# Reordering the mixers' element-wise work, the sample columns' convolution and the first attention loads in a hybrid decoder step

## What is computed

```python
h = rmsnorm(x); z = h @ w_in            # columns shared out among the mixers
# A forgetting attention, 4 heads x 64: causal for the prompt, and over 8192 paged keys for the samples
s = q @ k.T * scale + c_q - c_k         # c = cumsum(log forget gate)
# B RWKV-7: xm = sh + rw_mu * (prev - sh), r, k, v, w, a from xm, kk = k*rw_kk
kk = kk * rsqrt(max(sum(kk*kk), 1e-12)) # per head, then a scan with a matrix state
# C causal pooling with windows 2/4/8/16
# D glu = u1 * sigmoid(u2); y = depthwise conv (31 taps) + conv_b
yn = (y - mean) * rsqrt(var + 1e-5) * ln_g + ln_b
out = silu(yn) @ pw_out
x = x + concat(each mixer * silu(its gate)) @ w_out; y = rmsnorm(x)
```

## Time and profile before

| | |
|---|---|
| median of 3 runs | 1674.64 us (1670.19 to 1675.73) |
| the profiled execution: its time | 1666.86 us |
| its span from the first instruction to the last | 1665.1 us |
| mean granted clock of PE | 0.976 |
| PE busy | 1553.4 us, 93% |
| DVE busy | 987.7 us, 59% |
| ACT busy | 602.8 us, 36% |

### The profile page before, as it was taken

How to read it: one execution, slowest core, us unless ns; L and a number is a source line. 1 busy time by engine, 2 the same in 40 slices (tenths; PEclk the granted TensorE clock), 3 DMA queues, 4 the chain that set the end, 5 groups by cost and what they waited for, 6 DMA issues and landing times.

```text
span 1665.1 us, 35933 instructions
## 1 busy us (share of the span) xinstructions
PE 1553.4 (93%) x14428; PEld 1152.3 (69%) x14428; DVE 987.7 (59%) x2382; ACT 602.8 (36%) x1235; POOL 82.1 (5%) x97
## 2 busy tenths in 40 slices
PE   7979999999999999997777999998999999999998
PEld 5867778888887888886644666667887865444443
DVE  5689764767457666678375666634554549333333
ACT  3234342443434441334444565543333353010001
POOL 1010000000000000000000000000000003222220
PEclk9999999999999999999879999999999999999999
DMA  6354473446544374344758746668575559999983
GB/s 225 116 189 160 163 280 129 154 142 235 198 134 158 111 262 143 112 159 157 237 197 241 198 142 187 176 202 245 170 220 177 185 197 357 358 337 353 354 314 132
DMA packets 184495, 341.71 MB, mean 205 GB/s; under 512 B 22213, under 2 KB 124101, under 8 KB 173638
## 3 DMA queue, kind: packets, MB, share of 16 engines
q1 hardware_dynamic: 167338, 256.88, 47.3%
q0 software_dynamic: 10496, 72.98, 11.7%
q10 hardware_dynamic: 6496, 9.56, 1.5%
HBM read 286.13 MB, written 55.35 MB: 205 GB/s over the span
## 4 chain that ended last, share of the span: by engine, by line
PE 45%; ACT 3%; DMA 2%; issue 1%; DVE 1%; SPq 1%; ACTq 0%; DVEq 0%
PE psum L1323 24%; PE psum L1017 5%; PE psum L1269 4%; PE psum L1197 4%; PE psum L1283 4%; PE psum L1628 2%; PE psum L1044 1%; PE psum L1531 1%; DMA big<-lfD 1%; DMA big<-zT 1%; ACT big L1712 1%; PE psum L1031 1%; SPq L817 0%; DMA big<-rkv 0%; ACT big L1964 0%
## 5 line engine op out<-in xcount | busy, mean ns | idle before, releaser
L1044 PE MATMUL psum<-big 128*128 128x256 f32 (+1 forms) x1920 | 438.7, 386 | 11.2 <-DVE big L2085 9.3
L1044 PEld LDWEIGHTS psum<-big 128*128 128x128 f32 x1920 | 367.3, 192 | 70.4 <-DVE big L2085 10.1
L1725 ACT ACTIVATE zst<-psum 128x256 f32<-128x256 f32 (+1 forms) x336 | 126.7, 384 | 442.5 <-PE psum L1044 440.5
L1323 PE MATMUL psum<-big 64*64 64x64 f32 (+4 forms) x5440 | 256.1, 270 | 16.0 <-issue 9.3
L1323 PEld LDWEIGHTS psum<-big 64*64 64x64 f32 (+2 forms) x5440 | 176.8, 131 | 100.8 <-issue 74.7
L1044 PE MATMUL psum<-big,wbuf 128*128 128x256 f32 (+1 forms) x768 | 181.3, 384 | 0.0
L1044 PEld LDWEIGHTS psum<-big,wbuf 128*128 128x128 f32 x768 | 146.2, 191 | 23.0 <-issue 0.4
L2269 DVE SCALAR_TENSOR_TENSOR big<-big,pars 128x512 f32<-128x512 f32 x240 | 161.0, 744 | 0.4
L979 POOL DMA_INDIRECT big<-in_cache_v,pidx x64 | 68.2, 1065 | 687.3 <-PE psum L1283 474.1
L1197 PE MATMUL psum<-big 64*128 64x512 f32 (+3 forms) x320 | 74.9, 578 | 18.4 <-DMA big<-zT 12.3
L1712 ACT ACTIVATE big<-big 128x512 f32<-128x512 f32 (+11 forms) x108 | 83.9, 803 | 11.2 <-DVE big L2345 7.5
(11 more groups left out here) (322 smaller groups left out, 2028.7 us busy)
## 6 DMA issues: line engine op xcount, KB each, us to landing
big<-in_k_pages SPq DMA_DIRECT2D x432, 128.0 KB, 2.3
big<-wS SPq DMA_DIRECT2D x36, 768.0 KB, 5.8
zst<-in_k_pages SPq DMA_DIRECT2D x80, 128.0 KB, 2.7
wS<-big SPq DMA_DIRECT2D x12, 768.0 KB, 5.7
wbuf<-in_w_pairs SPq DMA_DIRECT2D x18, 512.0 KB, 3.9
big<-in_w_pairs SPq DMA_DIRECT2D x18, 512.0 KB, 4.4
...
```

Source lines behind the costliest of these rows:

```text
L1044: last = nc.tensor.matmul(psum[:, bank, 0:wide(p) // 2], left(k), right(k), start=first and k == 0, stop=k == 3, skip_group_check=True)
L1323: return nc.tensor.matmul(out, l, r, start=start, stop=stop, skip_group_check=True)
L1725: nc.scalar.activation(parts_[:, U % 2, COPIED_TO[j], 0:n], psum[:, (0, 1, 2, 0, 1, 2, 3)[j], 0:n], ACT.Copy, scale=0.125 if i == U_QA els ...
```

## The change

It does five things. (1) Token shift: the term mu*prev is made by ACT (`shifted`, two Copy with a scale per row tensor, in the unit after), DVE keeps one multiply-add per row (`mix_pair` with `one_m_mu`) and does it after the unit's taps. (2) ACT also takes the gain of the next pass's inputs (a Copy with a scale of 512 columns in units 2 to 9; `normed` becomes two wide multiplications), the key norms' floor (`key_sums`, a Relu) and small copies for the samples; the Sigmoid of U_U2 comes after the first copy of unit 3, `lora_inputs` moves from unit 3 to unit 5. (3) The samples' convolution moves from pass 0, unit 3 to pass 1, unit 1 and is normalised with pass 1. (4) Pass 3 has its mean after unit 8 and its variance after unit 10 as the other passes, its state steps one unit earlier, `conv_root(3)` and `conv_silu(3)` inside unit 11, ahead of its last copies; `TAPS` is shared out anew. (5) The first attention loads are issued by SP in unit 10 of pass 3; `conv_gated(3)` comes after the first item's row maxima; `KEYS_AT` begins 10, 12, 14 in place of 8, 11, 13, `forget_sums` 0 and 1 come in items 7 and 10 in place of 5 and 7, and POOL's stores wait for later items. Rows of `ek` are ordered anew (`EK_ROWS`) so that the first loads find free rows.

```diff
-        MEAN_AT, VAR_AT = (8, 8, 8, 9), (10, 10, 10, 11)
+        MEAN_AT, VAR_AT = 8, 10
-        KEYS_AT = (8, 11, 13, 15, 17, 19, 21, 22, 23, 24, 25, 26, 27, 28, 29, 30)
+        KEYS_AT = (10, 12, 14, 16, 18, 20, 21, 22, 23, 24, 25, 26, 27, 28, 29, 30)
-        TAPS = ((0, 0, 5, 4, 4, 4, 6, 8, 0), (0, 0, 5, 4, 4, 4, 6, 8, 0), (0, 0, 5, 4, 4, 4, 6, 8, 0), (0, 0, 1, 1, 5, 5, 6, 7, 6))
+        TAPS = ((0, 0, 4, 4, 4, 4, 7, 8), (0, 0, 4, 5, 5, 5, 6, 6), (0, 0, 4, 5, 5, 5, 6, 6), (0, 0, 1, 5, 6, 7, 6, 6))
...
+            def first_columns():
+                sp.wait_ge(z_stored[0], z_stores(0, U_KA))
+                sp.wait_ge(z_stored[1], z_stores(0, U_QA))
+                sp.wait_ge(pool_stored, stores(3))
+                sp.wait_ge(v_stored, stores(3))
+                sp.wait_ge(nc_kept, 16)
+                sp.wait_ge(rw_stored, 128 * PASSES - 64)
+                kq_load(0, kq_in)
+                sp.dma_start(ck_first, ncD[:, 0:512].unsqueeze(0).to_broadcast([P, 4, 512])).then_inc(ck_in[0], 16)
...
                     if i == 10:
-                        store_scan_rows(p, 1)
                         if p + 1 < PASSES:
                             sp.wait_ge(pool_stored, stores(p))
                             wvf_load(p + 1, 1)
+                        if p == PASSES - 1:
+                            first_columns()
+                        store_scan_rows(p, 1)
...
+            pool.wait_ge(o_read, 9)
+            pool.dma_start(O['vE'], vtok[:, :, 0:256]).then_inc(st_stored, 16)
...
             for x in range(2):
+                pool.wait_ge(o_read, 12 + 2 * x)
                 pool.dma_start(O['kT'][x], zT[KA + x]).then_inc(st_stored, 16)
...
+            def key_sums(p):
+                for t in TILES:
+                    for h in HALVES:
+                        a_(kinv[:, t, half(p, h)], of_small(('key', p, t, h))[:, 0:wide(p) // 2], ACT.Relu, sr_act, bias=under)
+
+            def shifted(p, i):
+                act.wait_ge(z_add, adds_through(p, i))
+                act.wait_ge(halo_in, 3 * p + i - U_R + 1)
+                for r in range(2):
+                    a_(sig_w[:, r, 0:PT_W], ek[:, EK_ROWS[i - U_R] + r, 0:PT_W], ACT.Copy, mu_ready, scale=par7[:, 8 + 2 * (i - U_R) + r:9 + 2 * (i - U_R) + r])
...
             def lora_gates(p):
+                act.wait_ge(sh_done, mixed_through(p, MIX_V))
...
             def unit(p, i):
-                copies(p, i, 0, 2)
+                if i == 6:
+                    key_sums(p)
+                copies(p, i, 0, 1)
+                if i == 3:
+                    gate(p, U_U2, ACT.Sigmoid, u2d)
+                copies(p, i, 1, 2)
...
-                if i == 3:
-                    lora_inputs(p)
+                if i in (4, 5, 6):
+                    shifted(p, i - 1)
                 copies(p, i, 2, 3)
...
-                if i == 3:
-                    gate(p, U_U2, ACT.Sigmoid, u2d)
+                if i == 5:
+                    lora_inputs(p)
...
-                if i == 11 and p < 3:
+                if i == 11:
                     conv_root(p)
                 copies(p, i, 5, 6)
+                if 2 <= i < 2 + KT and p + 1 < PASSES:
+                    row = hb[(p + 1) % 2][:, i - 2, 0:PT_W]
+                    a_(row, row, ACT.Copy, gained, scale=par7[:, i - 2:i - 1])
...
+                if i == 11 and p == 3:
+                    conv_silu(p)
                 copies(p, i, 6, 7)
...
             def normed(p):
                 dve.wait_ge(rs_ready, 2 * p + 2)
+                dve.wait_ge(gained, KT * p)
                 for h in HALVES:
-                    for k in range(KT):
-                        row = hb[p % 2][:, k, half(p, h)]
-                        ins = v.scalar_tensor_tensor(row, row, par7[:, k:k + 1], rs[h], ALU.mult, ALU.mult)
-                        ch.mark(ins)
+                    row = hb[p % 2][:, :, half(p, h)]
+                    ch.mark(v.tensor_tensor(row, row, rs[h].unsqueeze(1).to_broadcast([P, KT, PT_W // 2]), ALU.mult))
...
             def mix_pair(p, i):
-                mix(p, 2 * (i - U_R), 2, sig_w[:, :, 0:PT_W])
+                at, n = EK_ROWS[i - U_R], 2 * (i - U_R)
+                dve.wait_ge(mu_ready, 2 * (3 * p + i - U_R + 1))
+                for r in range(2):
+                    row = ek[:, at + r, 1:1 + PT_W]
+                    v.scalar_tensor_tensor(row, row, one_m_mu[:, n + r:n + r + 1], sig_w[:, r, 0:PT_W], ALU.mult, ALU.add).then_inc(sh_done, 1)
...
                     if i in (3, 4, 5):
-                        mix_pair(p, i)
-                    if i == 3 and p == 0:
-                        sample_taps(0)
-                        sample_taps(1)
+                        mix_kept(p, i)
...
-                    if 2 <= i <= 8:
+                    if 2 <= i <= 7:
                         taps_at(p, i)
-                    if i == 8 and MEAN_AT[p] == 8:
+                    if i in (3, 4, 5):
+                        mix_pair(p, i)
+                    if i == 8:
                         centered(p)
...
-                    if j in (5, 7):
-                        forget_sums((j - 5) // 2)
+                    if j in (7, 10):
+                        forget_sums((j - 7) // 3)
```

264 lines of the change are left out of this document (144 added, 120 removed).

## The result

| | before | after |
|---|---|---|
| median | 1672.41 us (4 runs, 1664.34 to 1675.73) | 1627.35 us (4 runs, 1624.30 to 1629.30) |
| ratio to before | | 0.9736, 95% interval 0.9705 to 0.9766 |
| profiled execution | 1666.86 us | 1629.3 us |
| its span, PE's mean granted clock | 1665.1 us, 0.976 | 1627.4 us, 0.987 |

A forecast was written before the change was run, and what follows sets the result against it. PE, busy 93% of the span, was taken as the bound, so only its idle stretches and low clocks could be won: 9.6 + 4.0 - 0.9 + 1.2 + 9.0 + 7.6 + 11.1 = 41.6 us, forecasting 1633 us from the median, range 1614 to 1652.

The forecast's parts named there:

- Pass 0: Units 4 and 5: earlier Sigmoid and less DVE work remove holes of 2.59 and 6.67 us and low clock; net 9.6 us.
- Mean of pass 0: Pass 0's mean: unit 7 keeps 8 taps, its sums come later, hole 3.0 in place of 2.1: -0.9 us.
- Value weights: Their load, issued before the scan-row stores, removes the 2.88 us hole and 1.5 of low clock, less 0.4: 4.0 us.
- Passes 1 and 2: Means gain 2.0 us per pass, key norms wait about 1.4 per pass: +4.0 - 2.8 = 1.2 us.
- Pass 3: Earlier mean removes its 9.29 us hole and low clock, together 11.15, less 1.1 and a key wait of 1.0: 9.0 us.
- Start: Start of attention: early loads hidden, ACT's tail awaited instead; first transposes 12.8 us after PE's last product, not 20.4: 7.6 us.
- Items 5 to 12: Attention: waits of 5.64 us (forget rows) and 7.01 (key pages) go, 1.5 given back: 11.1 us, bounds 5 to 15.
- Rival (b): Attention: pages' wait moves to items 12 and 14, 1.5 us in each of six early steps: 1645; chance 0.10.
- (a): Projection: ACT-DVE handoffs cost 4 us more in each of four passes: 1649; chance 0.13.
- (c): Start of attention: `first_columns` held by a wait until unit 11 ends, 7.6 us less gain: 1641; chance 0.04.
- (d): Projection: ACT becomes the bound, PE pays its 35 us of added work; slower, 1687; chance 0.05.
- The list of holes: PE's idle stretches over 0.7 us in projection and attention, those that matter listed with releasers and summed to 52 us.

The follow-up runs named there:

- Experiment 1: Kernel before with unit 3's Sigmoid behind its first copy and one tap of pass 0 moved from unit 2 to unit 6: 1667.78 us, ratio 0.9965.
- Experiment 9: Changed kernel with the second part of the value weights' load put back behind the second tile's scan-row stores: 1634.43 us, ratio to before 0.9781.
- experiment 7: Changed kernel with taps 4, 4, 4, 6, 7, 6 in pass 0 and 5, 5, 4, 5, 6, 6 in passes 1 and 2: 1625.56 us.
- experiment 5: Changed kernel with ACT's list of pass 3's last unit reordered, and first scores waiting only for the first five copies: 1622.01 us, ratio to before 0.9706.
- experiment 4: Changed kernel with the loads of attention's first columns put back behind the projection: 1633.84 us, ratio to before 0.9778.
- experiment 6: Changed kernel with one unused 128 x 1 Sigmoid in ACT's unit 6 of every pass, loading the table early: 1621.54 us, ratio to before 0.9686.
- experiment 2: Kernel before with attention's items alone moved (key steps from item 10, first forget sums in items 7 and 10): 1660.37 us, ratio 0.9922.
- experiment 3: Changed kernel with attention's items put back (key steps from item 8, first forget sums in items 5 and 7): 1634.45 us, ratio to before 0.9777.
- experiment 10: Changed kernel with each of ACT's added shifts done twice, DVE's multiply-adds waiting for the second: 1627.80 us, ratio to before 0.9741.

## Why the prediction was right

**Pass 0 (9.6 predicted, 11.0 measured).** Experiment 1 shows the mechanism, one queue on DVE. The deductions came as summed: of 1.2 us for what ACT would be late with, 0.56 appeared in unit 4 and 0.68 at the low-rank products (1.45 for 0.77). Of the 1.4 us too many, 0.9 were there already when unit 4 began (96.79 to 95.92), where the prediction has no term (up to 30 us after ran at a granted clock of 0.84 and before at 0.72); and PE's busy time from there to unit 7 fell by 2.1 us in place of 1.56.

**Mean of pass 0 (-0.9).** The hole is 2.63 for a predicted 3.0: -0.5 to the mean, as forecast by size (-0.5 of -0.9). Another -0.5 came behind it, at a clock of 0.54 from 170.3 to 177.1, which the term left out; the six experiments that take 6.16 us there in place of 6.72 don't have it.

**Value weights (4.0).** Mis-sized: the hole is 1.20 and not 0.4. 1.7 us of hole and the 1.5 of low clock make 3.2 (the stretches of 1.8 and 0.5, with the keys' 0.96 in the latter). Experiment 9 returned the hole but not the clock, so that this part of the term is luck as much as cause.

**Passes 1 and 2 (1.2).** The means wait 0.70 in place of 2.92 (2.2, predicted 2.0), the keys 0.96 (predicted 1.4). I missed that the low-rank products wait 1.47 in place of 1.20. In pass 2 these make 1.0 us, where the timelines show 0.3; the rest I can't name. The profile's releaser of the key norms, "issue", is not the forecast ACT; but one tap fewer ahead of them removes the wait (experiment 7), so the chain named, taps before shift before squares, was right. Pass 3 lost 2.3 us up to its key norms: 0.80 there (predicted 1.0) and 1.28 at the samples' state (681.25). "The state steps one unit earlier" was costed at nothing, and its cover, DVE's queue, was not looked at.

**Pass 3 (9.0, or 10.0 from the key norms on).** 10.3 measured, 8.0 with what was lost up to the key norms. The 9.29 us at the mean became 1.13. This rests on the two traces alone: no experiment put pass 3's order back by itself, nor the samples' convolution.

**Start (7.6).** 6.7 measured. ACT's tail is what is late next, as said (5.49 for some 6, released by L1753), and experiment 5 shows it. That the hidden loads would take 12.3 us wherever they stand was wrong: behind the projection in the new order they cost PE 7.74 us (experiment 4), and the rest of their worth lies in DVE's wait for what is issued with them. The drain of 1.38 us that the Trainium skill (ScalarE: Activation LUTs, What ACT_TABLE_LOAD costs) adds to each switch isn't there: in experiment 6 the activation starts 0.01 us behind the load, and a sum with it would have put the first transposes 18.3 us behind PE's last product, where 12.8 were forecast and 13.7 measured. The Trainium skill (ScalarE: Activation LUTs, Table sets: the hidden batching unit) says that copies belong to every set, so that a table loaded early is still there after them; experiment 6 agrees (two copies of products between the load and the Sigmoids).

**Items 5 to 12 (11.1).** Right in mechanism and too low. Over attention alone the items bring 13.4 us in the kernel before (experiment 2) and 11.3 in the changed one (experiment 3); attention as a whole gained 15.3. The idle time that went is near the sum, 9.7 us in experiment 2 and 10.2 in all; what the middle of the forecast put at nothing is the low clock behind the two holes, 3.7 us in experiment 2 and 5.1 in all, which stood only in its upper bound of 15. K's and V's stores, not priced either, don't explain the surplus: put back, they open a hole that the kernel before didn't have. Rival (b) is real at 1.83 us for one step and not at six.

**Rivals.** (a) did not show: in after no hole inside a unit of passes 1 to 3 is longer than the 0.96 us that before had too. (c) is out by the load's issue at 784.51. (d), ACT as the bound, did not come, and experiment 10 says that it wasn't near: twice the shifts cost nothing that can be measured.

**The sum.** 41.6 predicted against 44.5 at the ruler and 45.1 by the medians. The agreement is better than that of the parts: attention came 4.2 us higher and the start 0.9 lower, and in single stretches the clock's scatter is 1 to 2 us. The list of holes that opens the prediction adds up to 54.3 us and not 52; nothing hangs on it. That I went from the median and not from the profiled execution (7.8 us apart) was the better choice, and the ruler tells why: the profiled execution of before had the shortest stretch behind attention of all fourteen traces, 549.0 us.
